# Six of ten norms fused with the rounding and splitting of their output, one tile of the second unit begun chunk by chunk, and the order of the closing sums changed

## The reference

```python
x = layer_norm(x, ln_in_g, ln_in_b)
for l in range(2):
    mod = (silu(c) @ ada_w[l] + ada_b[l]).reshape(b, 3, 3, 1, 1024)
    h = modulate(x, mod[:, 0, 0], mod[:, 0, 1])          # x * (1 + scale) + shift
    y = swiglu_ffn(h, ffn1_w_in[l], ffn1_w_out[l])
    x = layer_norm(ALPHA * x + 0.5 * mod[:, 0, 2] * y, ln_g[l, 0], ln_b[l, 0])
    h = modulate(x, mod[:, 1, 0], mod[:, 1, 1])
    y = mixers(h @ mix_w_in[l]) @ mix_w_out[l]           # ssd, forgetting attention, short convolution
    x = layer_norm(ALPHA * x + mod[:, 1, 2] * y, ln_g[l, 1], ln_b[l, 1])
    h = modulate(x, mod[:, 2, 0], mod[:, 2, 1])
    y = swiglu_ffn(h, ffn2_w_in[l], ffn2_w_out[l])
    x = layer_norm(ALPHA * x + 0.5 * mod[:, 2, 2] * y, ln_g[l, 2], ln_b[l, 2])
```

## Time and profile before

| | |
|---|---|
| median of 3 runs | 3715.49 us (3715.28 to 3717.51) |
| the profiled execution | 3713.76 us, its span 3712.0 us |
| TensorE matmul busy | 3640.5 us (98% of the span), 19444 instructions |
| VectorE busy | 2271.7 us (61%) |
| ScalarE busy | 1712.3 us (46%) |
| GpSimd busy | 742.8 us (20%) |
| HBM read | 393.48 MB, 107 GB/s over the span |

### The profile page before, as it was taken

One profiled execution on the slowest core, in us unless ns is written; L12 is line 12 of the kernel. 1 busy time (PEld: TensorE's weight loads), 2 busy tenths in 40 slices (PEclk: granted clock), 3 DMA queues, 4 the chain that ended last, 5 costly groups with the idle time before them and its releaser, 6 DMA issues.

```text
span 3712.0 us, 48979 instructions
## 1 busy us (share of the span) xinstructions
PE 3640.5 (98%) x19444; PEld 3076.7 (83%) x19444; DVE 2271.7 (61%) x2757; ACT 1712.3 (46%) x2654; POOL 742.8 (20%) x755
## 2 busy tenths in 40 slices
PE   9999999999999999999999999999999999999998
PEld 7888877888888888788888689888888888988886
DVE  6555766744564567777545488685655466875345
ACT  4444434543454454346433269554544244853233
POOL 3000302200120012032003447450000143642001
PEclk9999999999999999999999999999999999999999
DMA  6554212344344432124422111223332112322221
GB/s 258 192 217 159 90 60 77 149 151 168 133 175 164 160 137 91 51 98 170 147 109 84 42 38 36 77 80 135 115 136 102 52 52 74 78 85 91 102 92 67
DMA packets 71794, 417.37 MB, mean 112 GB/s; under 512 B 9120, under 2 KB 12320, under 8 KB 30624
## 3 DMA queue, kind: packets, MB, share of 16 engines
q1 hardware_dynamic: 70320, 408.19, 30.8%
q10 hardware_dynamic: 1264, 6.29, 0.4%
HBM read 393.48 MB, written 2.10 MB: 107 GB/s over the span
## 4 chain that ended last, share of the span: by engine, by line
PE 87%; DVE 7%; ACT 2%; issue 2%; DMA 1%; POOL 1%; SPq 0%; DVEq 0%; ACTq 0%; POOLq 0%
PE ps L2224 26%; PE ps L2225 25%; PE ps L2226 25%; PE ps L2973 2%; PE ps L3016 2%; DVE x_lat L3443 1%; DVE x_lat L3454 1%; DVE rstd_lat L3431 1%; PE ps L2951 1%; DMA raw<-ffn_in 1%; PE ps L2952 1%; DVE w_lo L3112 1%; PE ps L2710 1%; DVE x_lat L3387 0%; DVE h_lo L3464 0%
## 5 line engine op out<-in xcount | busy, mean ns | idle before, releaser
L2224 PE MATMUL ps<-h_hi,w_lo 128*128 128x512 f32 (+2 forms) x2872 | 1078.0, 375 | 24.4 <-DVE h_lo L3464 15.4
L2226 PE MATMUL ps<-h_hi,w_hi 128*128 128x512 f32 (+2 forms) x2872 | 1062.7, 370 | 0.0
L2225 PE MATMUL ps<-h_lo,w_hi 128*128 128x512 f32 (+1 forms) x2800 | 1037.0, 370 | 0.0
L3112 DVE TENSOR_TENSOR w_lo<-raw,w_hi 128x2048 fp32r<-128x2048 f32 (+3 forms) x250 | 530.9, 2124 | 651.3 <-ACT w_hi L1428 651.2
L1428 ACT ACTIVATE w_hi<-raw 128x2048 fp32r<-128x2048 f32 (+4 forms) x259 | 452.1, 1746 | 924.4 <-PE ps L2226 905.4
L2224 PEld LDWEIGHTS ps<-h_hi,w_lo 128*128 128x128 f32 (+1 forms) x2872 | 540.7, 188 | 134.3 <-DVE h_lo L3464 24.9
L2226 PEld LDWEIGHTS ps<-h_hi,w_hi 128*128 128x128 f32 (+1 forms) x2872 | 540.4, 188 | 94.4
L2225 PEld LDWEIGHTS ps<-h_lo,w_hi 128*128 128x128 f32 x2800 | 527.4, 188 | 87.4 <-issue 0.5
L2224 PE MATMUL ps<-hid_hi,w_lo 128*128 128x512 f32 (+1 forms) x1272 | 487.3, 383 | 3.7 <-DVE w_lo L3112 2.5
L2225 PE MATMUL ps<-hid_lo,w_hi 128*128 128x512 f32 (+1 forms) x1272 | 483.3, 380 | 0.0
L2226 PE MATMUL ps<-hid_hi,w_hi 128*128 128x512 f32 (+1 forms) x1272 | 482.9, 380 | 0.0
(11 more groups left out here) (527 smaller groups left out, 5828.2 us busy)
## 6 DMA issues: line engine op xcount, KB each, us to landing
raw<-ada SPq DMA_DIRECT2D x113, 1024.0 KB, 4.8
raw<-ffn_in SPq DMA_DIRECT2D x87, 1024.0 KB, 6.7
raw<-mlp_in SPq DMA_DIRECT2D x32, 1024.0 KB, 4.8
...
```

The source lines that it names most:

```text
L2224: eng.matmul(out, lo_w, hi_x, start=first, stop=False, skip_group_check=True)
L2225: eng.matmul(out, hi_w, lo_x, start=False, stop=False, skip_group_check=True)
L2226: return eng.matmul(out, hi_w, hi_x, start=False, stop=last, skip_group_check=True)
L3112: eng.tensor_tensor(w_lo[:, slot, 0:ln.width], raw[:, slot, 0:ln.width], w_hi[:, slot, 0:ln.width].bitcast(F32), ALU.subtract).then_inc(s_ ...
```

## The change

It has two parts.

At the six norms with one stream on both sides (`singly`), VectorE no longer scales x first. `gained` multiplies a centred chunk by the next stage's gain and by the reciprocal root at once, into sq_h; ScalarE's `rounded` adds the shift and rounds to h_hi; `split_chunk` adds the shift and subtracts h_hi, to h_lo. All three go by single chunks. ScalarE's and GpSimd's unrounded h are gone. x is scaled afterwards, by pairs of chunks (`x_scaled`): five of the eight instructions right behind the last chunk, three behind the third unit's steps of the next stage; GpSimd then gives x its gain and shift. On TensorE unit 1's second tile is begun in part 0, chunk by chunk: the two passes with w_hi run right after unit 0's matmuls of a chunk, the pass with w_lo runs at the end, in the place of all three. For this ScalarE rounds that half of unit 1's weights after chunk 1 and the other half after chunk 7. There are 5 empty matmuls instead of 11. In a mixer, the small tables that lie where the reciprocal root does wait until x is scaled.

At all ten named norms the matmul with chunk 6's squares moves from `totals_begun` to `close`, behind chunk 7's sum.

```diff
@@ BUSY, number()
 BUSY = (1, 2, 8, 0, 0)
+BUSY_SINGLY = (1, 2, 2, 0, 0)
...
+            if nm.next:
+                nm.next.behind = nm
+            nm.singly = bool(nm.name and nm.next and len(nm.streams) == len(nm.next.streams) == 1)
@@ GpSimd
+            def singly(norm):
+
+                eng.wait_ge(s_vec, w.vec + 7 * len(norm.streams))
+                for part in norm.parts:
+                    x = X[part.st]
+                    _, _, g, b = affine(norm, part.st)
+                    for k in range(DC):
+                        eng.wait_ge(s_n32, part.n32 + k // 2 + 1)
+                        eng.tensor_scalar(x[:, k, part.cs], x[:, k, part.cs], g[:, k:k + 1], b[:, k:k + 1], ALU.mult,
+                                          ALU.add).then_inc(s_xa, 1)
@@ ScalarE
+            def second_unit(ln, h):
+
+                slot, c = (ln.g0 + 1) % 2, weight_half(ln, h)
+                if h:
+                    eng.wait_ge(s_tile, ln.t0)
+                    raw_ready(eng, slot, ln.g0 + 1, 0)
+                eng.activation(w_hi[:, slot, c], raw[:, slot, c], ACT.Copy).then_inc(s_whi if h else s_whi2, 1)
...
+            def rounded(norm, part, k0, k1):
+
+                b = affine(norm, part.st)[1]
+                for k in range(k0, k1):
+                    eng.wait_ge(s_v, part.v0 + k + 1)
+                    eng.activation(H[part.st][0][:, k, part.cs], sq_h[part.st][:, k, part.cs], ACT.Identity,
+                                   bias=b[:, k:k + 1]).then_inc(s_nhi, 1)
+
+            def singly(norm):
+
+                first, second = norm.parts
+                eng.activation(eps_t[:, 3:4], eps_t[:, 0:1], ACT.Sqrt)
+                square_last(norm, 0)
+                mean_squared(norm, 0)
+                deviation(norm, 0)
+                eng.wait_ge(s_vec, w.vec + 7 * len(norm.streams))
+                rounded(norm, first, 0, 2)
+                second_unit(norm.next, 1)
+                rounded(norm, first, 2, 4)
+                square_last(norm, 1)
+                rounded(norm, first, 4, 6)
+                mean_squared(norm, 1)
+                rounded(norm, first, 6, DC)
+                second_unit(norm.next, 0)
+                deviation(norm, 1)
+                rounded(norm, second, 0, DC)
@@ ScalarE, mixer(), in front of a_head
+                eng.wait_ge(s_n32, mx.x.behind.parts[-1].n32 + DC // 2)
@@ TensorE, totals_begun() and close()
-                eng.wait_ge(s_sq, w.sq + 4 * ns)
-                eng.matmul(ps[:, B_SQ, 0:HALF], by_d[:, :], squares_of(norm, part.st)[:, DC - 2, c], start=False,
-                           stop=False, skip_group_check=True)
...
                 eng.matmul(sum_of(j), by_d[:, :], X[part.st][:, DC - 1, c], start=False, stop=True,
                            skip_group_check=True).then_inc(s_total, 1)
+                eng.wait_ge(s_sq, w.sq + 4 * len(norm.streams))
+                eng.matmul(ps[:, B_SQ, 0:HALF], by_d[:, :], squares_of(norm, part.st)[:, DC - 2, c], start=False,
+                           stop=False, skip_group_check=True)
                 eng.wait_ge(s_sq7, part.nidx + 1)
@@ TensorE, after_norm()
+                def rounded_weights_mm(u, q, part, k):
+
+                    hi, lo = chunk(ln, part.st, k)
+                    slot, ws = (ln.g0 + u) % 2, slice((q * ln.kc + k) * P, (q * ln.kc + k + 1) * P)
+                    out = ps[:, tile_bank(ln, u * ln.tpu + q, part.st), part.cs]
+                    eng.matmul(out, w_hi[:, slot, ws], lo[:, part.cs], start=k == 0, stop=False, skip_group_check=True)
+                    eng.matmul(out, w_hi[:, slot, ws], hi[:, part.cs], start=False, stop=False, skip_group_check=True)
+
+                def remainders_mm(u, q, part, k):
+
+                    slot, ws = (ln.g0 + u) % 2, slice((q * ln.kc + k) * P, (q * ln.kc + k + 1) * P)
+                    eng.matmul(ps[:, tile_bank(ln, u * ln.tpu + q, part.st), part.cs], w_lo[:, slot, ws],
+                               chunk(ln, part.st, k)[0][:, part.cs], start=False, stop=k == ln.kc - 1,
+                               skip_group_check=True)
+
...
-                            if k in [g[0] for g in GROUPS]:
-                                if n == 0 and not before_it:
-                                    busy(BUSY[GROUP_OF[k]])
-                                eng.wait_ge(s_nlo, len(GROUPS) * p.idx + GROUP_OF[k] + 1)
+                            if n == 0 and not before_it and k in [g[0] for g in GROUPS]:
+                                busy((BUSY_SINGLY if norm.singly else BUSY)[GROUP_OF[k]])
+                            if p in norm.parts and norm.singly:
+                                eng.wait_ge(s_nlo, p.lo0 + k + 1)
+                            elif k in [g[0] for g in GROUPS]:
+                                eng.wait_ge(s_nlo, p.lo0 + GROUP_OF[k] + 1)
                             if len(ln.streams) > 1 and n + 1 == len(parts) and k >= DC - 2:
                                 pair(0, p, k, (0,))
                                 continue
                             pair(0, p, k)
+                            if n == 0 and norm.singly and k:
+                                if k == 1:
+                                    eng.wait_ge(s_whi, ln.g0 + 2)
+                                    rounded_weights_mm(1, 1, p, 0)
+                                rounded_weights_mm(1, 1, p, k)
                             if wide > 1 and n + 1 == len(parts) and k == DC - 2:
                                 continue
                             if p in norm.parts and k == 3 and closing:
...
                         for k in range(DC) if wide > 1 else ():
-                            pair(1, p, k, (1,))
+                            if n == 0 and norm.singly:
+                                remainders_mm(1, 1, p, k)
+                            else:
+                                pair(1, p, k, (1,))
@@ VectorE, linear() and, the same call, mixer()
                         third_unit(ln)
+                        if ln.behind and ln.behind.singly:
+                            x_scaled(ln.behind, range(5, 8))
                         ada_of(ln, 0)
@@ VectorE, apply()
-                    halves = j == 0 and norm.next and norm.next.halved is not None
-                    if halves:
-                        second_unit_half(norm.next, 0)
-                    elif j == (len(parts) - 1 if both_next(norm) or three else 0) and norm.next:
+                    if j == (len(parts) - 1 if both_next(norm) or three else 0) and norm.next:
                         ahead(norm.next, 1, 2)
                     if j == 0 and len(parts) > 1:
                         inverse(norm, 1)
-                    if halves:
+
...
+            def gained(norm, j, k):
+
+                part = norm.parts[j]
+                eng.wait_ge(s_rstd, 2 * part.nidx + 2)
+                eng.wait_ge(s_u, len(GROUPS) * part.nidx + GROUP_OF[k] + 1)
+                eng.scalar_tensor_tensor(sq_h[part.st][:, k, part.cs], X[part.st][:, k, part.cs],
+                                         affine(norm, part.st)[0][:, k:k + 1], rstd[part.st][:, part.cs], ALU.mult,
+                                         ALU.mult).then_inc(s_v, 1)
+
+            def split_chunk(norm, j, k):
+
+                part = norm.parts[j]
+                hi, lo = H[part.st]
+                eng.wait_ge(s_nhi, DC * part.idx + k + 1)
+                eng.wait_ge(s_v, part.v0 + k + 1)
+                eng.scalar_tensor_tensor(lo[:, k, part.cs], sq_h[part.st][:, k, part.cs],
+                                         affine(norm, part.st)[1][:, k:k + 1], hi[:, k, part.cs].bitcast(F32), ALU.add,
+                                         ALU.subtract).then_inc(s_nlo, 1)
+
+            def x_scaled(norm, pairs):
+
+                for n in pairs:
+                    part, j = norm.parts[n // 4], n % 4
+                    x = X[part.st][:, 2 * j:2 * j + 2, part.cs]
+                    eng.wait_ge(s_v, part.v0 + 2 * j + 2)
+                    eng.tensor_tensor(x, x, rstd[part.st][:, part.cs].unsqueeze(1).broadcast_to([P, 2, HALF]), ALU.mult)\
+                       .then_inc(s_n32, 1)
+
+            def singly(ln, norm):
+
+                last_tile(ln, 0)
+                if quarters_done(ln, 6) < 4:
+                    split_quarters(norm.next, quarters_done(ln, 6), 4)
+                deviation(norm, 0)
+                centred(norm, 0, 0)
+                centred(norm, 0, 1)
+                inverse(norm, 0)
+                eng.wait_ge(s_vec, w.vec + 7 * len(norm.streams))
+                for j in range(2):
+                    if j:
+                        centred(norm, 1, 0)
+                        centred(norm, 1, 1)
+                    gained(norm, j, 0)
+                    gained(norm, j, 1)
+                    for k in range(DC):
+                        split_chunk(norm, j, k)
+                        if k % 2 == 0 and k + 2 < DC:
+                            centred(norm, j, k // 2 + 2)
```

(9 more changed lines are left out.)

52 lines of the change are left out of this document (29 added, 23 removed).

## The result

The changed kernel takes 3722.21 us (median of 20 runs, 3718.86 to 3725.09), the kernel before, in the same session, 3715.2 us (median of 20, 3711.19 to 3718.78). The ratio is 1.0021, with a 95% interval of 1.0015 to 1.0027: slower by 7.0 us where 8.3 was forecast. The profiled execution's span is 3717.9 us, 5.9 over before.

A forecast was written before the change was run, and what follows sets the result against it. VectorE's own order was taken to bound both parts of a fused norm. Six norms 3.9, third units 2.4, ffn2_in_1_0 1.1, last norm 0.6, two streams 0.3: +8.3 on 3715.49 gives 3723.8 us, range 3716.5 to 3731.

The forecast's parts named there:

- The new form at 0.48: On VectorE, each gained and split_chunk of 256 columns lasts 0.48 us and delays the next by 0.40; bounds 0.41 and 0.50.
- Part 0: First part of a fused norm: VectorE splits the first chunk 0.6 us sooner, the last at 412.9 instead of 411.75.
- the three waits of 0.37, 0.68 and 0.37: In part 0, VectorE waits for ScalarE's rounding at the first chunk, chunk 4 and the last chunk, in us.
- The fused norm +0.65: Each of the six norms with one stream on both sides takes about 0.65 us more; bounds -1.6 and +1.3.
- all six look alike: The six fused norms behave alike, so the forecast followed only the first, before mix_x_0.
- The third units: Behind the norms, five x_scaled delay VectorE's half for TensorE's third unit: 0.2 us in four, 0.8 before each of two mixers.
- The cover of the mixers: VectorE work lost in the mixers is made up over 4 units of mix_x: cost nothing; without cover, 2 to 4 us.
- The stall in ffn2_in_1_0: TensorE's fourth unit there waits 1.1 us for VectorE, which has x_scaled and two products in front; range 0.4 to 1.6.
- The order: Chunk 6's squares moved to the close at ten norms: gain 0 to 0.05; last norm +0.6, two-stream norms +0.3 together.
- The lock: Rival: each x_scaled before the third unit's half waits for a GpSimd instruction, 11 us more, 3735 us; chance 0.10.
- Nothing but the order: Rival: the interleaving changes no end, since VectorE is as late as before; 3716 us, chance 0.05.
- The fill pays: Rival: in fused norms the interleaved matmuls fill TensorE's idle time, 12.6 us less, 3703 us; chance 0.08.

The follow-up runs named there:

- e3: The changed kernel with TensorE's order of matmuls and empty matmuls put back to that of before, without the interleaving; ratio to before 1.0022.
- e6: The changed kernel with last_tile(1) on VectorE two chunks earlier, behind the split of chunk 1; ratio to before 1.0014.
- e11: The kernel before with TensorE's interleaving, and VectorE's half 1 of the second unit's remainders moved in front of part 0's last split; 3706.44 us, ratio 0.9979.
- e8: The changed kernel with x_scaled cut to 8 of its 256 columns, so the output is wrong in size; ratio to before 1.0015.
- e4: The changed kernel with each fused norm's last three x_scaled moved behind the fourth unit's split and the second unit's evacuation on VectorE; ratio to before 1.0020.

## Why the prediction was nearly right

**What bounds a fused norm: right.** VectorE's order does. e3 (other matmul order, same end), e6 and e11 (other VectorE order, same matmuls, other end) show it.

**The new form at 0.48 with 0.40 from start to start: right** (403.00 to 403.40 and all through).

**Part 0: right in kind, high by 0.2 to 0.3.** In the front's clock (after started its norm at 396.49, before at 396.94, so add 0.45) the chunks are all split at 412.7, forecast 412.9 (the prediction's own terms add up to 402.16 + 9.1 + 1.42 + 0.08 = 412.8); half 1 ends at 417.1, forecast 417.35; part 1's first chunk is at 419.3, forecast 419.6; TensorE is free at 418.4, forecast 418.6. The mis-sized term is ScalarE: 0.60 was the rounding with a scale and a bias; the new one has only a bias and takes 0.51. So the three waits of 0.37, 0.68 and 0.37 were, by the same count from start to start, 0.32, 0.57 and 0.26 (0.24, 0.49 and 0.18 in the brackets). The middle one, the one that I had named, is the one that mattered (e6). I noted it as a term and did not see that it could be had back by moving one instruction.

**The fused norm +0.65: measured +0.20 before mix_x_0 and +0.60 to +0.69 elsewhere** (without the third unit's wait), 3.48 for the six against 3.9. The nearness is luck in part. The recorded sum for part 1 slipped: 419.67 + 96 x 0.12 + 0.7 + 0.1 is 432.0, not 432.3, so by its own terms a norm is +0.35, and the third unit, whose half it had ready at 432.5 either way, waits 0.5 and not 0.2; the total of 8.3 stays. And of the 3.48 the order is 0.9, which the prediction had at nothing. Without it a norm is +0.43 on average.

**The first norm isn't like the others: the step "all six look alike" failed.** Before, it was 0.4 longer than the rest (34.69; 34.28 to 34.31 for the other five), as the first chunk came 7.59 us after the first sum, not 7.16 as in the norms before ffn1_in_1_0 and mix_x_1. In after it comes at 7.04 to 7.05 in all three, so the first norm gets 0.54 at the head, the other two 0.12. In front of ffn2_in_0_0, ffn2_in_1_0 and mlp_in_1_0 it even comes 0.14 later, 7.14 to 7.15 for 7.00 to 7.01. The forecast's 0.6 at the head holds for the norm that it was read from.

**The third units: 0.8 + 1.6 forecast, 0 + 0.32 measured. The step that failed: the half w_lo comes too late for TensorE.** It ended at 431.45 before mix_x_0 and TensorE began at 431.51, a wait of 0.13 (0.19 before mix_x_1); in ffn2_in_1_0 it ended 0.5 before its need, and e8 gains nothing there. Two terms were too high. The first x_scaled began at 426.9 in the front's clock, not 427.5; and the five took 3.09, 0.60 each from start to start, with nothing on top for GpSimd beside them, for which I had added 0.35 (in the other five norms one of the five took 0.20 longer). They were done at 430.0 in the front's clock. The prediction had named that as a sign of being wrong ("before 430.7"), and in this term it was.

**The cover of the mixers: wrong.** I costed it at nothing ("4 units of mix_x to make up") and put 0.8 a mixer on the third unit; it came as 0.13 and 0.19 there, and 0.72 and 0.54 behind, most of it at the v weights. The total for the mixers, 1.6 in both, is right by two misses that cancel.

**The stall in ffn2_in_1_0: 1.1 forecast, 1.18 measured**; e4 and e8 take it away. The products (4.68) and x_scaled (2.08) stand there in front of the split, and TensorE's fourth unit behind it and the gate step (L3256):

```profile
1691.58 2.08 DVE L3621 TENSOR_TENSOR x_lat<-x_lat,rstd_lat 128x512 f32<-128x512 f32 x3
1693.59 4.68 DVE L3289 TENSOR_TENSOR products<-raw,c_row 128x2048 f32<-128x2048 f32 x2
1698.19 2.28 DVE L3187 TENSOR_TENSOR w_lo<-raw,w_hi 128x2048 fp32r<-128x2048 f32 x1
1701.13 0.50 PE L2274 MATMUL ps<-h_hi,w_lo 128*128 128x512 f32 x1 [1.02 <-DVE val_t L3256]
```

**The order: right sign, wrong place.** 0.4 at the last norm (0.6 forecast), about 0.1 in each of the three norms that lead to two streams or have them, and 0.9 in the fused norms, where it was costed at 0 to a gain of 0.05. The step that failed: the squares "end when they did". They do only if the pair in front has nothing to wait for; the sum of x waits for `last_tile`.

**The signs.** The new form at 0.48, a wait of about 1 us at part 1's first chunk (0.92) and one at the fourth unit of ffn2_in_1_0 came. The third unit 29.6 behind the last tile did not in the norm followed (29.16), and part 0 was split 10.5 us after the reciprocal's end, not 10.8.

**The rivals.** The lock at full weight: no. At most one of the five x_scaled took 0.20 longer beside GpSimd, where that rival had 0.5 for each. "Nothing but the order": no. "The fill pays" failed for the reason given against it, a chain that got no shorter; e11 shows its other branch, with before's own VectorE instructions and the half in the hole. The clock stayed at 1.00, the 2.4 GHz level, through the norm, its wait of 0.9 included:

```profile
402.35:431.51 29.16, 27.72 (x209) 25.81 (x207) 27.12 (x53) 12.86 (x23) 3.80 (x3) 1.00 0.11 37
```
